# Router logits from the residual tiles, with norm weight, shift and root applied around the product

## What is computed

```python
x = x + g * y                                             # y: the mixer's output projection
h2 = rms_norm(x, norm_ffn_g[l]) * (1.0 + sc2) + sh2       # rms_norm: x * rsqrt(mean(x*x) + EPS) * g
# expert_choice_ffn(h2, ...)
aff = jax.nn.softmax(jnp.einsum('bnd,de->bne', h, w_router).astype(jnp.float32), axis=-1)
gate, idx = lax.top_k(jnp.swapaxes(aff, 1, 2), capacity)
xe = jax.vmap(lambda hb, ib: hb[ib])(h, idx)
```

## Time and profile before

| | |
|---|---|
| median of 3 runs | 1749.31 us (1748.43 to 1749.66) |
| profiled execution | 1748.36 us, its span 1746.4 us |
| PE busy | 1668.2 us (96%) |
| DVE busy | 1350.3 us (77%) |
| ACT busy | 1046.7 us (60%) |
| chain that ended last | PE 91%, DVE 5%, DMA 2%, ACT 1% |

### The profile page before, as it was taken

How to read it: one execution, slowest core, us unless ns; L and a number is a source line. 1 busy time by engine, 2 the same in 40 slices (tenths; PEclk the granted TensorE clock), 3 DMA queues, 4 the chain that set the end, 5 groups by cost and what they waited for, 6 DMA issues and landing times.

```text
span 1746.4 us, 22137 instructions
## 1 busy us (share of the span) xinstructions
PE 1668.2 (96%) x8353; PEld 1382.7 (79%) x8361; DVE 1350.3 (77%) x1293; ACT 1046.7 (60%) x985; POOL 146.2 (8%) x137
## 2 busy tenths in 40 slices
PE   6999999999999379999999999999999999999995
PEld 3689987879888268888888888888888888888884
DVE  4566544318864788998899889989988998898897
ACT  5252221236641247777777777777777777777775
POOL 3002200002100010110100101101101001011010
PEclk9999999999999689999999999999999999999998
DMA  9216521111232669999999999999999999999996
GB/s 346 66 40 192 172 96 49 49 49 50 87 133 101 225 230 377 382 371 398 375 381 390 372 385 389 370 392 384 370 398 374 381 391 370 386 389 369 393 382 237
DMA packets 204441, 492.83 MB, mean 282 GB/s; under 512 B 5716, under 2 KB 18808, under 8 KB 204392
## 3 DMA queue, kind: packets, MB, share of 16 engines
q1 hardware_dynamic: 187616, 435.30, 66.9%
q0 software_dynamic: 13248, 47.09, 8.8%
q10 hardware_dynamic: 3528, 9.75, 1.4%
HBM read 471.07 MB, written 21.05 MB: 282 GB/s over the span
## 4 chain that ended last, share of the span: by engine, by line
PE 91%; DVE 5%; DMA 2%; ACT 1%; issue 0%; ACTq 0%; DVEq 0%; POOL 0%; POOLq 0%
PE ps L1124 88%; PE ps L1571 2%; DMA moda<-in_w_mod 1%; PE ps L1522 1%; DVE topi L2099 1%; DVE topv L2098 1%; DVE affT L2101 1%; DVE ring L2182 1%; PE ps L1459 0%; DVE wl L2149 0%; DMA xe<-ffn_in,idx_e 0%; PE ps L1143 0%; DVE wol L1981 0%; DVE ygT L1893 0%; DVE raw L1891 0%
## 5 line engine op out<-in xcount | busy, mean ns | idle before, releaser
L2149 DVE TENSOR_TENSOR wl<-ring,wh 128x2048 fp32r<-128x2048 f32 x384 | 877.4, 2289 | 104.8 <-ACT wh L1068 104.4
L1068 ACT ACTIVATE wh<-ring 128x2048 fp32r<-128x2048 f32 x384 | 737.1, 1921 | 279.4 <-PE ps L1124 279.4
L1124 PE MATMUL ps<-wh,xeh 128*128 128x512 f32 x1024 | 403.9, 394 | 0.3 <-DVE xel L2129 0.3
L1124 PE MATMUL ps<-wh,xel 128*128 128x512 f32 x1024 | 400.8, 391 | 0.0
L1124 PE MATMUL ps<-wl,xeh 128*128 128x512 f32 x1024 | 276.6, 392 | 0.0
L1124 PEld LDWEIGHTS ps<-wl,xeh 128*128 128x128 f32 x1024 | 192.4, 188 | 41.6
L1124 PEld LDWEIGHTS ps<-wh,xel 128*128 128x128 f32 x1024 | 192.5, 188 | 41.4
L1124 PEld LDWEIGHTS ps<-wh,xeh 128*128 128x128 f32 x1024 | 192.2, 188 | 40.7 <-DVE xel L2129 0.8
L1124 PE MATMUL ps<-wh,hidh 128*128 128x512 f32 x512 | 202.7, 396 | 0.0
L1124 PE MATMUL ps<-wh,hidl 128*128 128x512 f32 x512 | 200.1, 391 | 0.0
L1124 PE MATMUL ps<-wl,hidh 128*128 128x512 f32 x512 | 138.3, 392 | 0.0
(11 more groups left out here) (373 smaller groups left out, 2044.1 us busy)
## 6 DMA issues: line engine op xcount, KB each, us to landing
ring<-in_w_gate_e SPq DMA_DIRECT2D x64, 2048.0 KB, 9.2
ring<-in_w_up_e SPq DMA_DIRECT2D x64, 2048.0 KB, 9.0
ring<-in_w_down_e SPq DMA_DIRECT2D x64, 2048.0 KB, 10.5
mbw<-in_w_mod POOLq DMA_DIRECT2D x32, 512.0 KB, 5.1
hpr<-in_w_in SPq DMA_DIRECT2D x12, 1024.0 KB, 5.3
moda<-in_w_mod SPq DMA_DIRECT2D x3, 2048.0 KB, 20.2
xs<-in_x POOLq DMA_DIRECT2D x8, 512.0 KB, 8.4
wor<-in_w_out SPq DMA_DIRECT2D x2, 2048.0 KB, 7.7
```

The costliest lines, as they stand in the source:

```text
L1068: act.activation(whv[m % 4], eview(m), ACT.Copy).then_inc(hi_done, 1)
L1124: return pe.matmul(o, l, r, start=start, stop=stop)
L2149: dve.tensor_tensor(wlv[m % 4], eview(m), whv[m % 4].bitcast(F32), ALU.subtract).then_inc(lo_done, 1)
```

## The change

The router's product is taken on `x2` instead of `h2`. `to_features` transposes `x2` and waits for `x2_ready`. Its weights `wra` are the router's, multiplied by (1 + sc2) * norm_ffn_g for each feature; a row `brow` holds for each partition the sum of shift times router weight, and a matmul with ones (`router_bias`) adds it up over the partitions and leaves it on all of them. Three small loads on POOL's queue (`vec3`) and one transpose (`router_columns`) bring the three vectors into column form. `router_logits` multiplies the first seven tiles' logits with the reciprocals of the roots and adds the row. The last tile's logits go to bank 4, its transposed halves are copied by DVE and by ACT, its `keep_clock` calls are cut from 38 and 9 to 7, and its shift (`shifted(NT - 1)`) and its `features_out` come later. `h2` is still made and sent for the experts.

```diff
@@ PE
+        def rbank(t):
+            return 5 if t < NT - 1 else 4
             def to_features(t):
-                pe.wait_ge(h2_ready, t + 1)
+                pe.wait_ge(x2_ready, t + 1)
...
-                                        h2[:, t % 2, k * P:(k + 1) * P], ident[:])
+                                        x2[t % X2][:, k * P:(k + 1) * P], ident[:])
             def route(t):
-                pe.wait_ge(h2_c, t + 1)
                 if t == 0:
-                    pe.wait_ge(op_in, 16 * 5)
-                    pe.wait_ge(ym_ready, 4)
+                    pe.wait_ge(vcol_ready, 3)
+                if t < NT - 1:
+                    pe.wait_ge(h2_c, t + 1)
+                else:
+                    pe.wait_ge(xt_free_v, NTC + NT + 1)
                 for k in range(KT):
+                    if t == NT - 1 and k == H:
+                        pe.wait_ge(h2_c, t + 1)
...
+            def router_columns():
+                pe.wait_ge(op_in, 16 * 8)
+                pe.wait_ge(ym_ready, 4)
+                pe.transpose(ps[:, 5, 256:256 + 3 * KT], vec3[:], ident[0:3 * KT, 0:3 * KT]).then_inc(vec_t, 1)
+            def router_bias():
+                pe.wait_ge(vcol_ready, 2)
+                mm(ps[:, 5, 384:384 + NE], ones[:], brow[:], True, True).then_inc(vec_t, 1)
+            router_columns()
             for t in range(3, NT):
...
                 if t == 3:
+                    router_bias()
                     to_features(0)
...
-            keep_clock(0, ident[:], ident[:], 38)
             to_features(NT - 1)
-            keep_clock(0, ident[:], ident[:], 9)
+            keep_clock(0, ident[:], ident[:], 7)
             route(NT - 1)
@@ POOL
+            for i, v in enumerate((modrows[0, 2 * D:3 * D], norm_ffn_g[0], modrows[0, D:2 * D])):
+                pool.dma_start(vec3[i * KT:(i + 1) * KT, :], v.rearrange("(k p) -> k p", p=P)).then_inc(op_in, 16)
...
                     pool.wait_ge(h2_ready, t - X2 + 1)
+                    pool.wait_ge(h2_t, t - X2 + 1)
@@ ACT
+            feature_copy(NT - 1)
             act.activation(stat[:, 3, 0:1], epsc[:], ACT.Exp)
-            features_out(NT - 1)
-            feature_copy(NT - 1)
             act.wait_ge(ex_arg, 1)
             act.activation(eaff[:], eaff[:], ACT.Exp).then_inc(ex_done, 1)
+            features_out(NT - 1)
@@ DVE
             def normed(t):
...
-                    dve.wait_ge(h2_t, t - 1)
...
+                if t < NT - 1:
+                    shifted(t)
+            def router_weights():
+                dve.wait_ge(vec_t, 2)
+                link(dve.tensor_copy(cc[:].rearrange("p i k -> p (i k)"), ps[:, 5, 256:256 + 3 * KT]))
+                dve.tensor_tensor(wrb[:], wr[:], cc[:, 2].unsqueeze(2).to_broadcast([P, KT, NE]), ALU.mult)
+                link(dve.scalar_tensor_tensor(out=cc[:, 0], in0=cc[:, 0], scalar=1.0, in1=cc[:, 1], op0=ALU.add,
+                                              op1=ALU.mult))
+                dve.tensor_reduce(brow[:], wrb[:].rearrange("p k e -> p e k"), AX.X, ALU.add).then_inc(vcol_ready, 1)
+                dve.tensor_tensor(wra[:], wr[:], cc[:, 0].unsqueeze(2).to_broadcast([P, KT, NE]),
+                                  ALU.mult).then_inc(vcol_ready, 1)
+            def router_logits():
+                dve.wait_ge(vec_t, 3)
+                dve.wait_ge(rt_done, NT - 1)
+                link(dve.tensor_copy(crow[:], ps[:, 5, 384:384 + NE]))
+                link(dve.tensor_tensor(lgs[:], ps[:, 5, 0:NT * NE].rearrange("p (n e) -> p n e", n=NT),
+                                       stat[:, 2, 0:NT].unsqueeze(2).to_broadcast([P, NT, NE]), ALU.mult))
+                link(dve.tensor_tensor(lgs[:], lgs[:], crow[:].unsqueeze(1).to_broadcast([P, NT, NE]), ALU.add))
...
             for t in range(3, NT):
+                if t == 3:
+                    router_weights()
                 stream_tile(t)
+                if t == NT - 1:
+                    router_logits()
+                    dve.wait_ge(h2_t, NT)
+                    dve.tensor_copy(h2T[:, t % 2, 0:H], ps[:, 6, :].rearrange("p (k t) -> p k t", k=H)).then_inc(xt_free_v, 1)
...
             dve.wait_ge(rt_done, NT)
+            c7 = ORDER[NT - 1]
+            link(dve.scalar_tensor_tensor(out=lgs[:, c7], in0=ps[:, 4, c7 * NE:(c7 + 1) * NE], scalar=stat[:, 2, c7:c7 + 1],
+                                          in1=crow[:], op0=ALU.mult, op1=ALU.add))
...
             last.then_inc(aff_ready, 1)
+            shifted(NT - 1)
             dve.wait_ge(aff_t, 1)
```

More of the change, by code:

```diff
@@ L261, in hybrid_block @@
         topm = ot("topm", [P, NE])
+        vec3 = ot("vec3", [3 * KT, P])
+        cc = ot("cc", [P, 3, KT])
+        wra = ot("wra", [P, KT, NE])
+        wrb = ot("wrb", [P, KT, NE])
+        brow = ot("brow", [P, NE])
+        crow = ot("crow", [P, NE])
+        lgs = ot("lgs", [P, NT, NE])
         gained = at(TAIL + 9280, "gained", [P, D])
@@ L607, in _ @@
             pool.wait_ge(h2_ready, 6)
+            pool.wait_ge(h2_t, 6)
             pool.dma_start(g2row[:], modrows[0, 3 * D:4 * D].partition_broadcast(P)).then_inc(gains_in, 16)
@@ L1012, in feature_copy @@
                     act.wait_ge(rt_done, t - 1)
-                act.activation(h2T[:, t % 2], two(6, 8).rearrange("p (k t) -> p k t", k=KT),
+                k0 = 0 if t < NT - 1 else H
+                act.activation(h2T[:, t % 2, k0:], two(6 if k0 == 0 else 7, 8).rearrange("p (k t) -> p k t", k=KT - k0),
                                ACT.Copy).then_inc(h2_c, 1)
@@ L1459, in to_features @@
                     last = pe.transpose(ps[:, 6 + k // 4, k % 4 * P:(k % 4 + 1) * P],
-                                        h2[:, t % 2, k * P:(k + 1) * P], ident[:])
+                                        x2[t % X2][:, k * P:(k + 1) * P], ident[:])
                 last.then_inc(h2_t, 1)
             def route(t):
-                pe.wait_ge(h2_c, t + 1)
                 if t == 0:
-                    pe.wait_ge(op_in, 16 * 5)
-                    pe.wait_ge(ym_ready, 4)
+                    pe.wait_ge(vcol_ready, 3)
[3 more added lines that the diff above has]
+                    pe.wait_ge(xt_free_v, NTC + NT + 1)
                 for k in range(KT):
-                    last = mm(ps[:, 5, ORDER[t] * NE:(ORDER[t] + 1) * NE], h2T[:, t % 2, k], wr[:, k, :],
+                    if t == NT - 1 and k == H:
+                        pe.wait_ge(h2_c, t + 1)
+                    last = mm(ps[:, rbank(t), ORDER[t] * NE:(ORDER[t] + 1) * NE], h2T[:, t % 2, k], wra[:, k, :],
                               k == 0, k == KT - 1)
                 last.then_inc(rt_done, 1)
+            def router_columns():
[6 more added lines that the diff above has]
+            router_columns()
             for t in range(3, NT):
@@ L2031, in normed, with shifted @@
                 dve.wait_ge(ss2_ready, t + 1)
-                link(dve.reciprocal(stat[:, 2, t:t + 1], stat[:, 1, t:t + 1]))
+                link(dve.reciprocal(stat[:, 2, ORDER[t]:ORDER[t] + 1], stat[:, 1, t:t + 1]))
                 if t >= 2:
                     dve.wait_ge(h2_out[t % 2], 16 * (t // 2))
-                    dve.wait_ge(h2_t, t - 1)
-                link(dve.scalar_tensor_tensor(out=h2[:, t % 2], in0=x2[t % X2][:], scalar=stat[:, 2, t:t + 1],
+                link(dve.scalar_tensor_tensor(out=h2[:, t % 2], in0=x2[t % X2][:], scalar=stat[:, 2, ORDER[t]:ORDER[t] + 1],
                                               in1=a2row[:], op0=ALU.mult, op1=ALU.mult))
+                if t < NT - 1:
+                    shifted(t)
+            def shifted(t):
                 dve.tensor_tensor(h2[:, t % 2], h2[:, t % 2], b2row[:], ALU.add).then_inc(h2_ready, 1)
-            dve.wait_ge(op_in, 16 * 5)
+            dve.wait_ge(op_in, 16 * 8)
             link(dve.scalar_tensor_tensor(out=a2row[:], in0=a2row[:], scalar=1.0, in1=ffng[:], op0=ALU.add,
@@ L2079, in _ @@
             dve.wait_ge(rt_done, NT)
-            lg = ps[:, 5, 0:NT * NE].rearrange("p (n e) -> p n e", n=NT)
-            link(dve.tensor_reduce(srt[:, 0, :], lg, AX.X, ALU.max))
-            dve.tensor_tensor(eaff[:], lg, srt[:, 0, :].unsqueeze(2).to_broadcast([P, NT, NE]),
+            c7 = ORDER[NT - 1]
+            link(dve.scalar_tensor_tensor(out=lgs[:, c7], in0=ps[:, 4, c7 * NE:(c7 + 1) * NE], scalar=stat[:, 2, c7:c7 + 1],
+                                          in1=crow[:], op0=ALU.mult, op1=ALU.add))
+            link(dve.tensor_reduce(srt[:, 0, :], lgs[:], AX.X, ALU.max))
+            dve.tensor_tensor(eaff[:], lgs[:], srt[:, 0, :].unsqueeze(2).to_broadcast([P, NT, NE]),
                               ALU.subtract).then_inc(ex_arg, 1)
```

## The result

The changed kernel took 1751.36 us (median of 20 runs, 1749.28 to 1753.37) beside 1748.97 us before (20 runs, 1746.85 to 1750.27): a ratio of 1.0015 with a 95% interval of 1.0009 to 1.0021, which is 2.6 us more. The profiled execution took 1752.35 us, its span 1750.5 us. In one run of e3 (1986 us, granted clock 0.81) and one of the kernel before beside it (5113 us) the program ran far longer; they are counted in the medians and left out of the ratios.

What follows compares the result with a forecast made beforehand. PE, without slack in the tile loop, was taken to bound the kernel: plus 7.9 (wait), plus 1.5 (clock), minus 8.8 (last tile) = +0.6 us, so 1749.31 becomes 1749.9 us, range 1747.6 to 1753.1.

Steps and rivals of the forecast that it cites:

- The three large terms: In the sum: PE's late transposes plus 7.9 us, the slow clock plus 1.5, the last tile's gain minus 8.8.
- transposes of t = 3 late: In pass t = 3, PE waits for `brow`; transposes start at 505.6 instead of 497.66, 7.9 us late (7.5 to 8.6).
- slow clock behind the wait: Behind PE's wait in t = 3, 2.6 to 3.4 us run at half speed, costing 1.5 us (0 to 3.4).
- tiles 3 to 7: In the loop after tile 3, PE has nothing from which to win its lateness back.
- last tile: Behind the loop, fewer idle matmuls and transposes needing only `x2_ready` gain 8.8 us (8.2 to 9.2).
- PE has no slack in the loop: From 498 to 566 us PE is busy 68.00 of 68.00; a microsecond lost there is one at the end.
- The first rival: The wait at `brow` does not reach the end; only the last tile counts: 1740.5 us, chance 0.09.
- DVE raises `vcol_ready` only behind the memset: In t = 3, DVE's memset ends at 504.40; four operations of 0.90 us put `brow` at 505.3.
- The clock falls in the wait and costs half the slow time: PE stands still some 7.6 us in t = 3; the clock drops to half, costing 1.3 to 1.7 us.
- The upper bound of 3.4 us lost: Top of the clock term behind the wait: the loss if the slow stretch takes twice the longer restart time.
- the second rival: Behind the wait the clock stays at half speed; with 12 us of it plus 5.1, 1754.4 us, chance 0.08.
- The loads of `x2`, `features_out` and the weights cost nothing: In the loop, these loads and copies start later but still arrive before they are needed: no cost.

Runs made afterwards that it cites:

- e3: Changed kernel with 31 matmuls of no use filling PE's wait ahead of the matmul of `brow`: 1749.05 us, ratio 1.0001 against the kernel before.
- e1: Changed kernel with DVE's five router-weight operations moved ahead of `stream_tile(2)`: 1741.54 us, ratio 0.996 against the kernel before.
- f3: Kernel before with only a PE wait added in pass t = 3, until DVE's nop behind `gated_low(5)`: 1751.58 us, ratio 1.0019.
- f1: e2 with 17 matmuls of no use in PE's wait ahead of `route(0)`: 1744.73 us, ratio 0.9981 against the kernel before.
- e2: Changed kernel with the matmul of `brow` moved from pass t = 3 to t = 4: 1749.76 us, ratio 1.0004 against the kernel before.
- e4: Kernel before with its idle matmuls behind the loop cut from 38 and 9 to 20 and 5: 1744.52 us, ratio 0.9975.

## Why the prediction was right, and where its sizes were off

The forecast was no change that can be told, at +0.6 us; measured were +2.6 (1.6 to 3.7), inside the range and, but for the very end of the interval, inside the 3.5 us that were called no change, though 20 runs of each are enough to tell it from zero. The three large terms were all missed in the same direction, by 0.35, 1.0 and 0.28, which is most of the distance from +0.6 to +2.29. So tile 3's `gained` came 10.75 us late and not 9.4, and the maximum 2.29 and not 0.6. The steps, by the stage's ruler:

| term | forecast | changed kernel | shown apart by |
|---|---|---|---|
| transposes of t = 3 late | +7.9 | 20.52 - 12.27 = +8.25 | e1 (wait gone), e3 (wait alone: 8.05), f3 (one for one) |
| slow clock behind the wait | +1.5 | 10.75 - 8.25 = +2.50 | e3 (2.70), f1 against e2 (4.10 for a shorter wait) |
| tiles 3 to 7 | 0 | +0.06 | |
| last tile | -8.8 | -8.52 | e4 (4.52 of it without the new router) |
| sum | +0.6 | +2.29 | |

- *PE has no slack in the loop.* Right: 58.50 us from tile 3 to tile 7 beside 58.44, and PE busy for 62.00 of 62.00 us. The first rival, a wait that is absorbed, is refuted by f3.
- *DVE raises `vcol_ready` only behind the memset.* Right. Its four operations took 1.02 us from 505.64 to 506.66 instead of 0.90; the reduction took 0.37 and not the 0.28 of the row it was priced by the earlier trace rows. From the end of the reduction to the transposes it was 507.16 - 506.66 = 0.50 instead of 0.3.
- *The clock falls in the wait and costs half the slow time.* Right as a mechanism. The term that was mis-sized is the length: I took the two restarts of the kernel before, 2.6 and 3.4 us, as the bounds of the likely value. 5.8 and 5.2 us came, and 8.7 in e2. Two samples of one profile were too few. The same two places, with the same instructions, stand in all ten profiles of this study. Behind the top-8 rounds, after 35.9 us without work, the slow stretch is 3.4 us in the kernel before, 5.9 in the changed one, and 3.2 to 5.9 over the ten. Near 29 us the clock had fallen in six of the ten, and the stretch is 2.6 (before) to 5.9 us (e1). The profile of the kernel before happened to give the shortest of all near 29 us and the third shortest behind the top-8 rounds. In the changed kernel's profile it lasts from 622.66 to 628.6; these are PE's first work there (a line of the timeline) and the two microseconds around its end (busy time by stretch):

```profile
622.66 0.47 PE L1542 MATMUL ps<-ident,topf 64*128 64x64 f32 x2 [35.86 <-DVEq L2172]
```

```profile
627.00:628.00 1.00, 1.00 (x4) 0.74 (x3) 1.00 (x2) 0.00 (x0) 1.00 (x2) 0.50 0.00 0
628.00:629.00 1.00, 1.00 (x5) 0.82 (x4) 1.00 (x1) 0.00 (x0) 0.53 (x1) 0.70 0.63 66
```

  Half of 2.6 to 5.9 would have made the term 1.3 to 3.0, and the measured 2.50 lies in it. It is a little less than half of 5.8, as 4.10 is of e2's 8.7: at the half clock a matmul of 512 columns starts 0.43 us behind the last one and not twice 0.23. The upper bound of 3.4 us lost, kept for the range, covers the changed kernel and not e2 (4.10). With these numbers the second rival, a clock that stays low, was nearer than its price of 12 us at half speed made it look: e2 went most of the way.
- *The last tile.* Right to 0.3 us. Both copies were covered, by 0.6 and 0.9 us where 0.8 and 0.9 were worked out; before its first small step DVE waited 0.34 for tile 6's product, which the working had left out. The new operation on 16 columns cost 583.78 - 583.39 = 0.39 instead of 0.20, 0.15 of it a wait of DVE for its own result.
- *The loads of `x2`, `features_out` and the weights cost nothing.* They wait for the same things in e1, where no loss is left in the stage but 1.05 us on PE. POOL issued tile 3's load at 509.69, 9.3 us ahead of `gained` at 518.95.

The clock of this case does as the Trainium skill has it (TensorE: Matmul & The Clock Gate, Part 1): activity releases the throttle, and the trace agrees, 1.00 through the filled waits of e3 and f1, 0.50 behind the empty ones of the changed kernel and of e2 (7.3 and 3.8 us); in the empty wait of 1.9 us in f3 it stayed at 1.00.

## What to carry to other kernels

Work that moves off one engine's path has a setup, and the place of the setup in the other engine's list decides its price: the same five operations cost 10.75 us behind the memset and 1.05 us when they stood 8.7 us earlier. Price a gap on TensorE by its length and by the slow stretch behind it, and take the spread of such stretches from more than one profile, not their mean from one, since the same code gave 3.2 to 5.9 us here; idle matmuls in the gap bought back 2.7 and 4.1 us here. Idle matmuls are themselves in the list, so after each change ahead of them count how far they outlast what they wait for: 18 and 4 too many were 4.5 us of this kernel before any edit to the router.

## What the runs showed of the hardware that was not expected

- The slow clock's length does not follow the length of the gap. Gaps of 7.3 us gave 5.8 and 5.2 us of work at half speed, one of 3.8 us gave 8.7, and the same restart after 35.9 us without work gave 3.2 to 5.9 in ten profiles.
- Nor does the length of a gap alone say whether the clock falls. It stayed up through the 1.9 us of f3 and the gap under 2 us in the earlier trace rows. In e1's profile it fell at 28.2 us, in a gap of 1.71 us (27.36 to 29.07) that has another of 1.29 us close ahead of it, and in the kernel before at 28.6, in a gap of 2.20 us at the same place.
- In e2 the engine was busy for 7.94 of 8.00 us from 506 to 514 and the clock stayed at the half all through. Its work there began with sixteen rows of the 16-column router product and eight transposes; whether this kind of work made the stretch longer was not tried, and stays open. That something beside the work decides as well is shown by the spread over ten profiles at a place where the work is the same.
- A semaphore on DVE's nop is raised before the instructions ahead of it have ended: near 500.1 in f3, when the instruction in progress ended at 501.30 and the next one at 501.90. So in f3 it did not mark the end of the work ahead of it, and the wait came out 1.6 us shorter than meant.
